# Thirteen series of zeroed products after the warm-up products of a decoder-trunk kernel's opening

## The reference

```python
h = rms_norm(x, norm_mix[l])
proj = h @ w_in[l]                       # 2048 x 5120
a = sliding-window attention; o = HGRN2 recurrence; cb * yc = short gated convolution
x = x + jnp.concatenate([a, o, cb * yc], axis=-1) @ w_out[l]
h = rms_norm(x, norm_ffn[l])
gate, up = jnp.split(h @ w_gate_up[l], 2, axis=-1)   # 2048 x 2*5632
x = x + (jax.nn.silu(gate) * up) @ w_down[l]
```

## Time and profile before

| | |
|---|---|
| median of 2 runs | 2555.9 us (2554.94 and 2556.87) |
| span of the profiled execution | 2553.7 us (its own time is known by this span alone) |
| TensorE products recorded | 19426 |
| TensorE busy | 2540.0 us, 99% of the span |
| VectorE, ScalarE, GpSimd busy | 58%, 40%, 13% of the span |
| DMA | 420.84 MB, mean 165 GB/s |

### The profile page before, as it was taken

One profiled execution on the slowest core, in us unless ns is written; L12 is line 12 of the kernel. 1 busy time (PEld: TensorE's weight loads), 2 busy tenths in 40 slices (PEclk: granted clock), 3 DMA queues, 4 the chain that ended last, 5 costly groups with the idle time before them and its releaser, 6 DMA issues.

```text
span 2553.7 us, 51052 instructions
## 1 busy us (share of the span) xinstructions
PE 2540.0 (99%) x19426; PEld 2512.5 (98%) x19426; DVE 1476.0 (58%) x2011; ACT 1016.8 (40%) x1412; POOL 330.7 (13%) x279
## 2 busy tenths in 40 slices
PE   9999999999999999999999999999999999999998
PEld 9999999999999999999999999999999999999998
DVE  6678787555554445555545787775555444555544
ACT  5454554333333333333334545443333333333333
POOL 3011003111110011111100200131111000111111
PEclk9999999999999999999999999999999999999999
DMA  6545445454455444444454554444444454444443
GB/s 232 171 159 183 157 141 170 157 164 164 164 172 165 156 165 164 164 164 165 164 165 165 176 173 152 141 165 165 164 164 164 165 167 162 164 164 164 166 165 136
DMA packets 116516, 420.84 MB, mean 165 GB/s; under 512 B 13840, under 2 KB 15120, under 8 KB 116368
## 3 DMA queue, kind: packets, MB, share of 16 engines
q1 hardware_dynamic: 109296, 397.72, 46.1%
q0 software_dynamic: 4112, 14.78, 1.8%
q10 hardware_dynamic: 3024, 7.16, 0.9%
HBM read 411.06 MB, written 11.87 MB: 166 GB/s over the span
## 4 chain that ended last, share of the span: by engine, by line
PE 97%; DVE 2%; ACT 1%; DMA 0%; issue 0%; DVEq 0%; SPq 0%
PE gp L1590 31%; PE gp L1592 31%; PE gp L1591 31%; PE mb L1646 1%; PE mb L1757 0%; PE mb L1770 0%; PE mb L1778 0%; DMA raw<-wstream 0%; PE mb L1655 0%; PE mb L1704 0%; DVE wlo L767 0%; PE mb L1721 0%; ACT sc L564 0%; ACT sc L562 0%; PE mb L1832 0%
## 5 line engine op out<-in xcount | busy, mean ns | idle before, releaser
L1590 PE MATMUL gp<-xh,whi 128*128 128x288 f32 x4096 | 1223.2, 299 | 0.5 <-DVE xl L1254 0.5
L1591 PE MATMUL gp<-xl,whi 128*128 128x288 f32 x4096 | 1208.3, 295 | 0.0
L1592 PE MATMUL gp<-xh,wlo 128*128 128x288 f32 x4096 | 1204.5, 294 | 0.0
L767 DVE TENSOR_TENSOR wlo<-raw,whi 128x1024 fp32r<-128x1024 f32 x754 | 987.4, 1343 | 364.9 <-ACT whi L427 361.4
L427 ACT ACTIVATE whi<-raw 128x1024 fp32r<-128x1024 f32 x754 | 769.2, 1052 | 587.6 <-PE gp L1592 558.0
L1590 PEld LDWEIGHTS gp<-xh,whi 128*128 128x128 f32 x4096 | 767.7, 187 | 7.6 <-issue 5.9
L1592 PEld LDWEIGHTS gp<-xh,wlo 128*128 128x128 f32 x4096 | 771.4, 188 | 0.0
L1591 PEld LDWEIGHTS gp<-xl,whi 128*128 128x128 f32 x4096 | 769.3, 188 | 0.6
L1590 PE MATMUL gp<-fh,whi 128*128 128x288 f32 x1408 | 416.7, 296 | 0.0
L1591 PE MATMUL gp<-fl,whi 128*128 128x288 f32 x1408 | 415.4, 295 | 0.0
L1592 PE MATMUL gp<-fh,wlo 128*128 128x288 f32 x1408 | 414.0, 294 | 0.0
(11 more groups left out here) (266 smaller groups left out, 1781.0 us busy)
## 6 DMA issues: line engine op xcount, KB each, us to landing
raw<-wstream SPq DMA_DIRECT2D x754, 512.0 KB, 4.2
s<-s_cache POOLq DMA_DIRECT2D x8, 512.0 KB, 10.6
hs_out<-s ACTq DMA_DIRECT2D x8, 512.0 KB, 3.4
caches_out<-caches POOLq DMA_DIRECT2D x8, 496.0 KB, 8.7
x<-x_in ACTq DMA_DIRECT2D x4, 576.0 KB, 8.7
kct<-kt_cache POOLq DMA_DIRECT2D x4, 512.0 KB, 5.0
vct<-v_cache POOLq DMA_DIRECT2D x4, 512.0 KB, 6.5
y_out<-x SPq DMA_DIRECT2D x3, 576.0 KB, 2.9
```

Of the source, the lines that this page charges most:

```text
L767: v.tensor_tensor(wlo[slot][:], raw[slot][:], whi[slot][:].bitcast(F32), ALU.subtract).then_inc(lo_ready, 1)
L1590: t.matmul(out, w_hi, mv_hi, start=first, stop=False)
L1591: t.matmul(out, w_hi, mv_lo, start=False, stop=False)
L1592: mm = t.matmul(out, w_lo, mv_hi, start=False, stop=end)
```

## The change

Two tiles are laid over the start and the last part of `wide`: `zero_a`, 128 x 512, and `zero_b`, 128 x 640, both of the rounded type. GpSimd clears both after `qz`, before it clears `acc2`, and counts them in `ones_set`; the three waits on that semaphore now ask for 7. After the 23 products of `mean_x`, TensorE makes thirteen series of rounded products of these zeroed tiles into `mb[0]` (one of the series into `mb[0]` and `mb[1]`): six of 14 products with 288, 280, 272, 264, 320 and 304 columns; five of 14 with 288 columns in which, one after the other, the stationary operand moves from place to place, the moving operand starts 16 columns later, is read at every second column, is read in two pieces of 144, and the result goes to column 64; one of 28 products of 64 rows each, alternately the lower and the upper half of the partitions; and one of 14 with a stationary operand from `zero_b`. The results are read by nothing. That is 196 products more; all else stays.

```diff
--- before.py
+++ after.py
@@ -199,6 +199,10 @@
         krx = sub(over, "krx", [P, TOK])
         UPW = 2 + SEQ + 6 * DEC_BATCH
 
+        warm = [wide[0], wide[1]]
+        zero_a = sub(warm, "zero_a", [P, 512], F32R)
+        warm[0] = wide[1] - 16 * 1024
+        zero_b = sub(warm, "zero_b", [P, 640], F32R)
         temp = area(23 * 1024)
 
         t = list(temp)
@@ -652,7 +656,7 @@
                 with a.Fori(1 - part, FF_PART[part] // 2) as i:
                     pair(i)
 
-            a.wait_ge(ones_set, 5)
+            a.wait_ge(ones_set, 7)
             a.activation(one_col[:, 1:2], eps[:], ACT.Copy)
             a.wait_ge(par_loaded, 16)
             a.wait_ge(lb_steps, 2 * DEPTH)
@@ -1305,7 +1309,7 @@
                     with v.Fori(1, 3) as i:
                         in_groups(i)
                 v.wait_ge(const_loaded, 16)
-                v.wait_ge(ones_set, 5)
+                v.wait_ge(ones_set, 7)
                 half_masks(l)
                 group(n4 + 6, 0, 2)
                 opening(l * HG_HEADS, 0)
@@ -1401,6 +1405,8 @@
             e.memset(eps[:], NORM_EPS).then_inc(ones_set, 1)
             e.memset(new_mask[:], NEG_BIG).then_inc(ones_set, 1)
             e.memset(qz[:], 0.0).then_inc(ones_set, 1)
+            e.memset(zero_a[:].bitcast(F32), 0.0).then_inc(ones_set, 1)
+            e.memset(zero_b[:].bitcast(F32), 0.0).then_inc(ones_set, 1)
             for s in (hp, cvp, ap_):
                 e.sem_inc(s.sem, s.start)
             PER = 1 + KC
@@ -1834,9 +1840,37 @@
                 mm.then_inc(at.sem, at.step("pvs"))
                 yield
 
-            t.wait_ge(ones_set, 5)
+            t.wait_ge(ones_set, 7)
             for _ in range(AWAKE):
                 t.matmul(mb[0][:, 0:P], mean_x[:], mean_x[:], start=True, stop=True)
+            za, zb = zero_a[:], zero_b[:]
+            for i in range(14):
+                t.matmul(mb[0][:, 0:288], za[:, 0:P], zb[:, 0:288], start=(i == 0), stop=(i == 13))
+            for i in range(14):
+                t.matmul(mb[0][:, 0:280], za[:, 0:P], zb[:, 0:280], start=(i == 0), stop=(i == 13))
+            for i in range(14):
+                t.matmul(mb[0][:, 0:272], za[:, 0:P], zb[:, 0:272], start=(i == 0), stop=(i == 13))
+            for i in range(14):
+                t.matmul(mb[0][:, 0:264], za[:, 0:P], zb[:, 0:264], start=(i == 0), stop=(i == 13))
+            for i in range(14):
+                t.matmul(mb[0][:, 0:320], za[:, 0:P], zb[:, 0:320], start=(i == 0), stop=(i == 13))
+            for i in range(14):
+                t.matmul(mb[0][:, 0:304], za[:, 0:P], zb[:, 0:304], start=(i == 0), stop=(i == 13))
+            for i in range(14):
+                t.matmul(mb[0][:, 0:288], za[:, P * (i % 4):P * (i % 4) + P], zb[:, 0:288], start=(i == 0), stop=(i == 13))
+            for i in range(14):
+                t.matmul(mb[0][:, 0:288], za[:, 0:P], zb[:, 16:304], start=(i == 0), stop=(i == 13))
+            for i in range(14):
+                t.matmul(mb[0][:, 0:288], za[:, 0:P], zb[:, 0:576:2], start=(i == 0), stop=(i == 13))
+            for i in range(14):
+                t.matmul(mb[0][:, 0:288].rearrange("p (a b) -> p a b", a=2), za[:, 0:P], zb[:, 0:320].rearrange("p (a b) -> p a b", a=2)[:, :, 0:144], start=(i == 0), stop=(i == 13))
+            for i in range(14):
+                t.matmul(mb[0][:, 64:352], za[:, 0:P], zb[:, 0:288], start=(i == 0), stop=(i == 13))
+            for i in range(28):
+                rows = slice(64 * (i % 2), 64 * (i % 2) + 64)
+                t.matmul(mb[i % 2][:, 0:TOK], za[rows, 0:P], zb[rows, 0:TOK], start=(i < 2), stop=(i > 25))
+            for i in range(14):
+                t.matmul(mb[0][:, 0:TOK], zb[:, 288:288 + P], zb[:, 0:TOK], start=(i == 0), stop=(i == 13))
             for l in range(DEPTH):
                 n4 = l * (SLABS // RING)
                 g = l * GROUPS
```

## The result

The changed kernel takes 2581.5 us (2581.48 and 2581.52 in its two runs) against 2555.9 (the middle of two executions that lie 1.9 us apart): a ratio of 1.0099, 95% interval 1.007 to 1.0129. The forecast was 2580.6, so no change by the 2% bound, and a cost of 1.0% that is clear of the spread. The span of the profiled execution is 2579.9 us, 26.2 over the one before.

What follows compares the result with a forecast made beforehand. TensorE was taken as the bound, so added work counts in full: 1.0 + 22.3 + 1.9 + 0.2 - 0.7 = 24.7 us, on 2555.9 giving 2580.6 us. The range was 2577 to 2586 us.

Steps and rivals of the forecast that it cites:

- the two rivals about form: Zeroed series: half rows one by one, strided series at double price, or both; 2582.4, 2582.5 or 2584.3 us; chance 0.22.
- the prediction's own sign of being wrong: Trace after: a series much over 2 us, half rows following each other, or work after 36 us changed by over 1 us.
- this term's upper end: Series reading every second column: reading twice the span could double its price, 1.9 us more.
- the distance of 2.2 us that was carried from span to median: Median of two runs over the profiled span of 2553.7 us, added again to the forecast span of 2578.4.
- TensorE as the bound, and the series on top of everything: TensorE, busy 2540.0 of 2553.7 us, has no idle time before the real products, so added work counts in full.
- the very limit that was set for it: Work after 36 us: prediction wrong if it has grown or shrunk by more than 1 us.
- The two clears: GpSimd clears of 512 and 640 columns before the burst: 0.46 and 0.56 us, together 1.0 us later start.
- The twelve whole series: After the burst: 168 products of 128 rows at 0.133 us each, 22.3 us.
- the row for pieces: Earlier-profile product of 128 columns read in eight pieces, 293 ns against 271 in one; used to take no extra.
- The half rows: Series of 28 half-row products: pairs run at the price of one, 1.9 us, plus 0.2 us for switching.
- Given back: Opening: the stop at the second slab, for `xl`, goes because real products begin later; 0.7 us less.
- The slow part of the burst: Early burst products at 0.215 us against 0.111, excess 2.7 us; may vary by 2.7 us either way, no change taken.

## Why the prediction was right, point by point

The path was right, and the time came out 0.9 us off, partly by luck. Of the two rivals about form, one came true: the strided series cost double. By itself that makes 2582.5 us, and the prediction's own sign of being wrong, a series that costs much over 2 us, is there at 3.56. The range held because it kept this term's upper end, and the forecast came so near because two smaller misses pulled the other way: 0.3 us more was given back, and the distance of 2.2 us that was carried from span to median was 0.6 too large.

- TensorE as the bound, and the series on top of everything: right. From the first real product on, the changed kernel does the same work in the same time but for the stops, 1.0 us less, the very limit that was set for it.
- The two clears, 1.0 us: measured 1.04, and 1.06 as the difference of medians when the burst doesn't wait for them. Missing from the prediction is that this holds only because the series stand behind it; alone, the clears cost next to nothing, as the stop at the second slab absorbs them.
- The twelve whole series, 22.3 us: measured 24.2 (26.24 less 2.04 for the half rows), which holds 0.2 of the switches into and out of the half rows. This is the mis-sized term. The step that failed is "I take the low end, because the row for pieces shows almost nothing". That row is a plain float32 product, whose price hardly moves even at stride 2 (242 to 254 ns), and it reads pieces of 16 columns, and 16 are nearly free for rounded ones while 1 and 2 are not. It also gave lengths of products with 32 and with 128 rows, and not distances from start to start. The upper end that I kept, 1.9 us, was the measured 1.7. Widths that add up to six times 288 cost what was summed, to 0.1 us (11.14 us against 11.17), though the price is not one line over all widths.
- The half rows, 1.9 us and 0.2 for the switches: measured 2.04 for the series, with 0.09 more before it and 0.11 after, 2.2 in all instead of 2.1. The pairs cost 14 x 0.131 = 1.8, and the switches 0.4, twice what was taken: the sum read one late start at each switch, and the product behind it is late as well. The kernel before has this too, 0.24 us instead of 0.13 behind the return of the earlier trace rows:

```profile
252.55 0.40 PE L1590 MATMUL gp<-xh,whi 128*128 128x288 f32 x1
252.79 0.29 PE L1591 MATMUL gp<-xl,whi 128*128 128x288 f32 x1
```

  The two products of a pair start 3 to 12 ns apart, as in the earlier trace rows.
- Given back, 0.7 us: measured 1.0 between the two profiled executions. The stop at the second slab, the one named, is 0.72 of it. Another 0.09 is no gain: the second product behind the burst is late in both kernels (0.22 us instead of 0.13), and in the changed one it lies in the first series. The remaining 0.2 are small delays, most of them in the third to the fifth slab.
- The slow part of the burst as a source of spread: right in kind. It lasted 3.3 to 6.1 us, and the burst with it 6.7 to 8.0 us in the traces.
- Over all, the series cost 1.8 us more than summed (1.7 the stride, 0.2 the switches) and 0.3 more was given back, hence 26.2 by the spans instead of 24.7. The medians differ by 25.6, so the forecast came out 0.9 low. The 0.6 between the two is no merit of the sum: 2555.9 is the middle of two executions, one from each of the groups told above. In the changed kernel and in all but one of the runs after it, the time lies 1.5 to 1.6 us over the span, and not 2.2; with 1.6 the forecast had been 2580.0, 1.5 low, still inside the range.
- The Trainium skill's distance for an isolated product, 122.5 ns at 288 columns ("TensorE: Matmul & The Clock Gate", "Back-to-back issue gap"): a record of a plain float32 product costs 242 ns, twice 121, which would agree if a record holds two passes over the columns; no run here shows that it does. It doesn't agree for rounded ones, at 131.7 to 133.3.

## What to carry to other kernels

Work put into the bound engine's order costs its own sum, and that sum can be read from neighbouring rows if the form is the same; a form that no row shows keeps its upper bound in the range, and a neighbour with longer pieces and of another type is no evidence for single elements. Small losses that every product shares can be worth more than a stop in an opening: 1.7 ns on 12288 products were 20 us, found because throwaway products cost less than the real ones. Measure a form at several places before calling its price the engine's.

## What the runs showed of the hardware that was not expected

- A rounded product whose moving operand comes in pieces of 1 or 2 columns, half of them skipped, costs 255 ns for 288 columns, and 132 to 136 from pieces of 4 on. For 144 columns stride 4 costs what stride 2 does, 133 and 132. A plain product costs 254 at stride 2 against 242 a record.
- The start of the moving operand counts: 131.7 ns on a 256-byte grid (and 64 and 96 bytes after it), 133.3 at 32, 128, 160, 192 and 224 bytes after it, 136 and 135 at 4 and 8 bytes. Why is not shown. The last series of the change, with its stationary operand off the grid, cost 133 with a moving operand on it, so the stationary one may count too; only that series says so.
- A rounded product of 288 columns costs 240 ns at the lower clock level, exactly 1/1.2 ns a column, but 131.7 and not 120 at the upper.
- A change between whole and half rows costs 0.2 us each way, half of it before the first product of the new form and half before the next. From plain to rounded products it costs nothing: the first rounded one starts 0.03 us after the last plain record and the next 0.22 later, together what 0.11 and 0.13 would be.
- One subtraction of `xl` on VectorE lasted 1.7 us instead of 0.51 in six of the 14 traces, near 18 us; the cause is not shown. Where nothing stands in front of the real products, it goes with the upper of two groups of execution times, 1.7 us apart.
